# Expert routing with integer indices read in place, one mask table, two expert tables, and the negation and the gates on ScalarE

## The reference, cut to what matters

```
top_s, top_i = lax.top_k(scores, PEER_TOPK)
cand = (top_s[..., 0, :, None] + top_s[..., 1, None, :]).reshape(..., 256)
best_s, best_j = lax.top_k(cand, PEER_TOPK)
i1 = take_along_axis(top_i[..., 0, :], best_j // 16); i2 = take_along_axis(top_i[..., 1, :], best_j % 16)
experts = i1 * PEER_KEYS + i2
gates = jax.nn.softmax(best_s, axis=-1)
act = gelu(einsum('td,tkd->tk', h, u_tab[experts])); out = einsum('tk,tkd->td', gates * act, v_tab[experts])
```

## Time and profile before

| what | value |
|---|---|
| time, median of 3 runs | 1670.06 us (1668.13 to 1670.81) |
| the profiled execution's own time | 1670.59 us |
| its span, first to last instruction | 1668.8 us |
| busy: PE, DVE, ACT, POOL | 1308.3, 1209.0, 432.8, 677.2 us |
| moved by DMA | 623.21 MB, of which gathers 536.90 MB |

### The profile page before, as it was taken

How to read it: one execution, slowest core, us unless ns; L and a number is a source line. 1 busy time by engine, 2 the same in 40 slices (tenths; PEclk the granted TensorE clock), 3 DMA queues, 4 the chain that set the end, 5 groups by cost and what they waited for, 6 DMA issues and landing times. The chain is left out here.

```text
span 1668.8 us, 15094 instructions
## 1 busy us (share of the span) xinstructions
PE 1308.3 (78%) x4636; PEld 732.2 (44%) x4636; DVE 1209.0 (72%) x2831; ACT 432.8 (26%) x1021; POOL 677.2 (41%) x791
## 2 busy tenths in 40 slices
PE   7794776977696697878878777889878788776786
PEld 6664432433354344544355434545345433332332
DVE  3834999865599978767589987867679975555555
ACT  3211331341233321224133332135123321111111
POOL 6002223686175253344333243434432235444441
PEclk9898998988798898988989888989989979999999
DMA  9006998969998899999999999999999989999998
GB/s 387 18 29 265 418 374 334 392 258 367 421 407 351 328 420 419 420 421 419 420 398 420 411 345 420 420 419 420 420 401 420 402 319 422 420 419 420 420 420 334
DMA packets 86050, 623.21 MB, mean 373 GB/s; under 512 B 9808, under 2 KB 9808, under 8 KB 10960
## 3 DMA queue, kind: packets, MB, share of 16 engines
q0 software_dynamic: 73728, 536.90, 78.9%
q1 hardware_dynamic: 12240, 85.33, 12.5%
HBM read 621.15 MB, written 1.05 MB: 373 GB/s over the span
## 5 line engine op out<-in xcount | busy, mean ns | idle before, releaser
L1348 PE MATMUL acc<-slot,diag 128*128 128x512 f32 x1780 | 870.1, 644 | 226.9 <-ACT diag L734 226.9
L458 POOL DMA_INDIRECT slot<-experts,idx x512 | 577.9, 1129 | 950.3 <-PE acc L1348 785.4
L1041 DVE CUSTOM_DVE_ANT_0 slot<-slot,h 128x1024 f32<-128x1024 f32 x512 | 611.8, 1226 | 273.1 <-DMA slot<-experts,idx 271.5
L1348 PEld LDWEIGHTS acc<-slot,diag 128*128 128x128 f32 x1780 | 358.1, 207 | 689.4 <-issue 419.8
L734 ACT ACTIVATE diag<-cst,ge 128x128 f32<-128x128 f32 x445 | 144.2, 391 | 187.0 <-DVE ge L760 185.8
L725 ACT ACTIVATE ge<-ge 128x4 f32<-128x4 f32 x129 | 26.5, 205 | 466.0 <-DVE ge L1041 465.1
L1318 PE MATMUL PB<-hT,ring 128*128 128x128 f32 x1024 | 126.2, 284 | 4.6 <-ACT hT L698 4.1
L1318 PEld LDWEIGHTS PB<-hT,ring 128*128 128x128 f32 x1024 | 122.8, 200 | 6.5 <-ACT hT L698 5.5
L719 ACT ACT_TABLE_LOAD x31 | 39.8, 1283 | 203.1 <-DVE rs L1000 203.1
L1059 DVE SCALAR_TENSOR_TENSOR xs<-slot,ge,xs 128x1024 f32<-128x1024 f32 x67 | 86.1, 1285 | 2.4
L725 ACT ACT_TABLE_LOAD x56 | 71.8, 1283 | 29.3 <-DVE ge L1041 28.4
(11 more groups left out here) (229 smaller groups left out, 1148.4 us busy)
## 6 DMA issues: line engine op xcount, KB each, us to landing
ring<-weights SPq DMA_DIRECT2D x32, 1152.0 KB, 9.5
ring<-weights SPq DMA_DIRECT2D x28, 1024.0 KB, 9.2
slot<-weights SPq DMA_DIRECT2D x12, 1024.0 KB, 22.2
slot<-experts,idx POOLq DMA_INDIRECT x512, 16.1
sml<-small SPq DMA_DIRECT2D x2, 1160.0 KB, 10.0
xs<-x SPq DMA_DIRECT2D x2, 512.0 KB, 8.1
out<-xs SPq DMA_DIRECT2D x4, 256.0 KB, 5.1
tabp<-tabs SPq DMA_DIRECT2D x2, 268.0 KB, 9.2
```

What stands on the lines that cost most here:

```text
L458: pool.indirect_dma_start(out=slot[:, E % SLOTS, :], out_offset=None, in_=experts, in_offset=bass.IndirectOffsetOnAxis(ap=idx[:, n % 2, e: ...
L1041: ins = dve.tensor_tensor_reduce(u, u, h2[:, n % 2, :], 1.0, 0.0, ALU.mult, ALU.add, d[:, i:i + 1])
L1348: ins = pe.matmul(acc[:, half, :], diag[:, d % DIAGS, :], slot[:, E % SLOTS, D + half * 512:D + half * 512 + 512], start=(E % PICKS == 0), ...
```

## The change

Each part of it is in `route` or beside it:

- The reference to one expert table is replaced by two, `experts0` and `experts1`, one for each layer, and `gather` takes the one of its step. The offset (L1015) goes; the multiply-add (L1014) writes the indices itself.
- `bj` is split by one bitwise AND with a constant pair of rows (240 and 15) instead of a shift and an AND. The constants are written by two memsets on POOL at the start. The first half is then 16 times i1's place, and the table that it is compared with holds 0, 16, ..., 240 for the first half and 0 to 15 for the second.
- The conversions to float (L1003, L1006) go: comparison and product read the uint32 tiles as they are.
- The negation (L1000) is done by ACT, ahead of its exponential; the last MAX8 itself signals `top_ready`.
- The gates (L1019) are done by ACT: it waits behind the exponential for DVE's reciprocal (`ginv_ready`), multiplies, and signals `gated`. DVE waits for `gated` in the first quad of every head.

```diff
-def trunk(nc, x, consts, small, tabs, weights, experts, out):
+def trunk(nc, x, consts, small, tabs, weights, experts0, experts1, out):
@@ POOL
+            pool.memset(parts[:, 0, :], (TOPK - 1) * TOPK)
+            pool.memset(parts[:, 1, :], TOPK - 1).then_inc(S["parts_ready"], 1)
...
+                src = experts[n // TILES]
...
-                        out=slot[:, E % SLOTS, :], out_offset=None, in_=experts,
+                        out=slot[:, E % SLOTS, :], out_offset=None, in_=src,
@@ ACT, route
                 act.wait_ge(S["top_ready"], R + 1)
+                link(act.activation(rs[:, 0:1], bs[:, 0, 0:1], ACT.Copy, scale=-1.0))
                 told(act.activation(bs[:, 1, :], bs[:, 0, :], ACT.Exp, bias=rs[:, 0:1],
                                accum_out=rs[:, 1:2]), "gexp_ready")
+                act.wait_ge(S["ginv_ready"], R + 1)
+                told(act.activation(gate[:, n % 2, h * TOPK:(h + 1) * TOPK], bs[:, 1, :], ACT.Copy,
+                               scale=rs[:, 2:3]), "gated")
@@ DVE, route
-                def best():
-
-                    told(dve.tensor_scalar(rs[:, 0:1], bs[:, 0, 0:1], -1.0, None, ALU.mult), "top_ready")
-
-                top16([(bs[:, 0, :], bj[:, 0, :], cand[:, 0, :], cand[:, 1, :])], best)
-                lag(dve.tensor_copy(tif[:, :, :], ti[:, :, :]))
-                lag(dve.tensor_scalar(bj[:, 1, :], bj[:, 0, :], 4, None, ALU.logical_shift_right))
-                link(dve.tensor_scalar(bj[:, 2, :], bj[:, 0, :], 15, None, ALU.bitwise_and))
-                link(dve.tensor_copy(bjf[:, :, :], bj[:, 1:3, :]))
+                top16([(bs[:, 0, :], bj[:, 0, :], cand[:, 0, :], cand[:, 1, :])], "top_ready")
+                if R == 0:
+                    dve.wait_ge(S["parts_ready"], 1)
+                link(tt(bj[:, 1:3, :], bj[:, 0, :].unsqueeze(1).to_broadcast([P, 2, TOPK]), parts[:, :, :],
+                        ALU.bitwise_and))
...
-                link(tt(hot, bjf[:, :, :].unsqueeze(3).to_broadcast(both),
-                        c_("iota").unsqueeze(1).unsqueeze(1).to_broadcast(both), ALU.is_equal))
-                link(tt(hot, hot, tif[:, :, :].unsqueeze(2).to_broadcast(both), ALU.mult))
+                place = c_("iota").rearrange("p (i a) -> p i a", i=2).unsqueeze(2).to_broadcast(both)
+                link(tt(hot, bj[:, 1:3, :].unsqueeze(3).to_broadcast(both), place, ALU.is_equal))
+                link(tt(hot, hot, ti[:, :, :].unsqueeze(2).to_broadcast(both), ALU.mult))
                 link(dve.tensor_reduce(ex[:, 0:2, :], hot, AX.X, ALU.add))
-                link(dve.scalar_tensor_tensor(ex[:, 2, :], ex[:, 0, :], float(KEYS), ex[:, 1, :], ALU.mult, ALU.add))
-                told(dve.tensor_scalar(idx[:, n % 2, h * TOPK:(h + 1) * TOPK], ex[:, 2, :], float(l * EXPERTS), None,
-                                       ALU.add), "routed")
+                told(dve.scalar_tensor_tensor(idx[:, n % 2, h * TOPK:(h + 1) * TOPK], ex[:, 0, :], float(KEYS),
+                                              ex[:, 1, :], ALU.mult, ALU.add), "routed")
                 dve.wait_ge(S["gexp_ready"], R + 1)
-                link(dve.reciprocal(rs[:, 2:3], rs[:, 1:2]))
-                link(dve.tensor_scalar(gate[:, n % 2, h * TOPK:(h + 1) * TOPK], bs[:, 1, :], rs[:, 2:3], None,
-                                       ALU.mult))
+                told(dve.reciprocal(rs[:, 2:3], rs[:, 1:2]), "ginv_ready")
@@ DVE, weigh
                 dve.wait_ge(S["gelu_ready"], G + 1)
+                if quad % PER_HEAD == 0 and quad < QUADS:
+
+                    dve.wait_ge(S["gated"], PH * n + quad // PER_HEAD + 1)
```

More of the change, by code:

```diff
@@ L42 @@
 QUADS = PICKS // GRP
+PER_HEAD = TOPK // GRP
 DIAGS = 6
@@ L53 @@
 for _name, _w in (("ident", P), ("mask", P), ("ones", P), ("band", 4 * P), ("prev", 64), ("first", 64),
-                  ("iota", TOPK), ("minus", HEADS), ("eps", 1)):
+                  ("iota", 2 * TOPK), ("minus", HEADS), ("eps", 1)):
     CONST[_name] = (_at, _at + _w)
@@ L194, in by_vector @@
     return E - by_tensor(E)
-def trunk(nc, x, consts, small, tabs, weights, experts, out):
+def trunk(nc, x, consts, small, tabs, weights, experts0, experts1, out):
     ctx = ExitStack()
     with ctx:
+        experts = (experts0, experts1)
         def sb(name, shape, dt=F32):
@@ L291, in trunk @@
         ti = sb("ti", [P, 2, TOPK], U32)
-        tif = sb("tif", [P, 2, TOPK])
+        parts = sb("parts", [P, 2, TOPK], U32)
         bs = sb("bs", [P, 2, TOPK])
         bj = sb("bj", [P, 3, TOPK], U32)
-        bjf = sb("bjf", [P, 2, TOPK])
-        ex = sb("ex", [P, 3, TOPK])
+        ex = sb("ex", [P, 2, TOPK])
         rs = sb("rs", [P, 4])
@@ L316, in trunk @@
                  "merged_ready", "x1_ready", "sumsq_x1", "rms_x1", "h2_ready", "h2T_psum",
-                 "h2T_ready", "qT_psum", "qTs_ready", "sc_ready", "top_ready", "gexp_ready", "routed",
+                 "h2T_ready", "qT_psum", "qTs_ready", "sc_ready", "parts_ready", "top_ready", "gexp_ready", "ginv_ready", "gated", "routed",
                  "dots_ready", "gelu_ready", "w_ready", "diag_ready", "expert_done", "added", "drained",
@@ L604, in dt, with gate_ @@
                 told(act.activation(base[:, 0, :], t_("ldt"), ACT.Exp), "dt_ready")
-            def gate(n):
+            def gate_(n):
                 act.wait_ge(S["pf_psum"], n + 1)
@@ L735, in weigh @@
                                    scale=ge[:, 2, G % 2, i:i + 1]).then_inc(S["diag_ready"], 1)
-            run(dict(dt=dt, normA=normA, gate=gate, ln=ln, bT=turn_b, z=z, glu=glu, qkn=qkn, v=v, att=att, pool=pool_, sq=sq,
+            run(dict(dt=dt, normA=normA, gate=gate_, ln=ln, bT=turn_b, z=z, glu=glu, qkn=qkn, v=v, att=att, pool=pool_, sq=sq,
                      merge=merge, x1=x1_, h2T=h2T, rp=rp, route=route), lambda n, quad: None, weigh)
@@ L965, in x1_, with top16 @@
                                                   ALU.mult), "h2_ready")
-            def top16(pairs, after=None):
+            def top16(pairs, found=None):
                 step = lag if len(pairs) == 2 else link
@@ L974, in top16 @@
                 for vals, inds, src, scratch in pairs:
-                    step(dve.max(vals[:, 8:16], scratch))
-                if after:
-                    after()
+                    ins = dve.max(vals[:, 8:16], scratch)
+                    if found:
+                        told(ins, found)
+                    else:
+                        step(ins)
                 for vals, inds, src, scratch in pairs:
@@ L1382, in const_pack @@
     put("first", first.reshape(P, -1))
-    put("iota", np.arange(TOPK)[None, :])
+    put("iota", np.concatenate([np.arange(TOPK) * TOPK, np.arange(TOPK)])[None, :])
     put("minus", -np.eye(P, HEADS))
@@ L1465 @@
     i = {k: np.asarray(v) for k, v in inputs.items()}
+    rows = [np.concatenate([i["peer_u"][l], i["peer_v"][l]], 1) for l in range(DEPTH)]
     small, tabs = small_pack(i)
@@ L1472 @@
         "weights": weight_pack(i),
-        "experts": np.concatenate([i["peer_u"], i["peer_v"]], 2).reshape(DEPTH * EXPERTS, 2 * D),
+        "experts0": rows[0],
+        "experts1": rows[1],
     }
```

## The result

| kernel | median | runs | against the kernel before, 95% interval |
|---|---|---|---|
| before | 1669.1 us | 1665.75 to 1670.81 | |
| changed | 1696.55 us | 1694.68 to 1698.05 | 1.0169 [1.0156, 1.0182] |

The change makes the kernel slower by 27.5 us; forecast were 1695.1 us and slower with 0.84. The profiled execution took 1697.49 us; its span is 1695.6, 26.8 more than before.

A forecast was written before the change was run, and what follows sets the result against it. DMA bounds most of the run, DVE's chain the stretches around the routings. First gather -0.9, step 0 +5.6, step 1 +7.0, steps 2 and 3 +12.8: +24.5 on 1670.59 gives 1695.1 us, range 1680 to 1707.

The forecast's parts named there:

- the four stretches: Around the routings: DVE waits for no gather for some 150 to 170 us, so its chain sets the run time.
- w: DVE's gate product, which waits for ACT's Gelu in a routing quad: forecast at t0 + 5.67, before t0 + 4.87.
- a hiding DMA: Rival: gathers in flight cover DVE's lag, only the first routing step counts, 1669.7 us; chance 0.06.
- The quad: One routing quad: 0.80 us longer, Gelu and its table load standing behind the gates, despite 1.15 us less DVE work.
- The quad with "bT": Quad of "route6", where ACT's copy of 512 columns is no longer covered: 1.40 us longer instead of 0.80.
- the rival with another 1.38 us of emptying: Rival: an exposed table switch on ACT costs 1.38 us more, 31 times, 1738 us; chance 0.02.
- The index work: DVE's routing chain: conversions, shift and AND save 0.48 us, the offset 0.21 us.
- The uint32 rival: Rival: a uint32 operand halves the rate of DVE's comparison and product, 0.69 us longer each, 1739 us; chance 0.03.
- Step 1's routing: Routing quads of step 1: 7 x 0.80 + 1.40, together +7.0 us.
- The bound of 1.8 less for this place: Step 1's routing, where DVE meets POOL's rotation-table run: earlier delays absorbed, four quads costing 1.4 us, not 3.2.
- The first gather: First routing step: the gather waiting for the index write comes 0.19 + 0.48 + 0.21 = 0.88 us earlier.
- The rival in which the Gelu's load goes first: Rival: ACT loads the Gelu's table ahead of its wait for the reciprocal, 1654.5 us; chance 0.07.

The follow-up runs named there:

- the gates alone: Kernel before with only the gates moved to ACT behind DVE's reciprocal, nothing else of the change; 1719.95 us, ratio 1.0288.
- seven copies: Kernel before with seven dead copies of 16 columns on ACT between exponential and Gelu of every routing step; 1702.69 us, ratio 1.0197.

## Why the prediction was right

**The bound.** DVE's chain set the pace in the four stretches: DVE's delay is found again in the span, +25.7 at the last routing quad and +26.8 at the end. The windows with 315 and 285 GB/s, though, are not ones in which DVE is full (13.24 and 13.60 of 20). The routings' last products w start inside them, at 966.41 and 1349.32, and in the first DVE then waits 6.1 us for PE's sums. The full DVE is in the windows ahead of them (19.34 at 940 us). The reading was right, the rows for it were not the best. The chance of 0.06 for a hiding DMA was fair: between kernels that are faster than before DMA does hide part.

**The quad.** Forecast +0.80, measured +0.85 from the MAX8 to w in the quad shown, +0.88 a quad in step 0 and +0.85 in step 2 (14.01 to 14.85). The reciprocal was right to 0.01. Two hand-overs on the path came 0.02 longer each than in the rows they were priced from (the reciprocal's end to ACT 0.10 for 0.08, the Gelu's start to w 0.31 for 0.29). That is the 0.05, and times 31 it is some 1.6 us. The quad with "bT" behind its routing step was 1.50 longer, where 1.40 was forecast.

**The table load.** It was the largest piece of the Gelu's lateness: without it the quads of step 0 are 1.28 us shorter, and the run 39.1. Its price when exposed is the same 1.28 as when hidden, and the next instruction starts 0.01 behind it, so the rival with another 1.38 us of emptying falls. "ScalarE: Activation LUTs" of the Trainium skill puts a switch at about 2.66 us; nothing here shows its second half.

**The index work.** Forecast were -0.48 and -0.21, together -0.69 a quad, measured -0.64 in step 0. The uint32 rival falls.

**Step 1's routing** was mis-sized: +7.0 forecast, +9.3 measured, and the excess lies in one quad, 27 (w's delay goes from 6.95 to 10.09, where 0.8 was forecast). The last of POOL's runs, which the prediction looked at, cost about what it did before (the AND 6.0 us over its usual 0.19, the multiply-add 6.4 over 0.17). DVE met it at the AND and not, as put there, at the product, and nothing was absorbed: POOL's run did not keep its place in time but began 6.2 us later itself (524.64 for 518.42). What was left out is the run before it. In the old kernel it began at 509.29, as the dot products (1.22 each) ended, and stood beside DVE's searches. In the changed kernel it began at 512.00, just ahead of the dot products, which took 1.65, 1.63, 1.64 and 3.00 us: 3.0 us more. That the run is what stretched them is read from the timelines; no experiment took this one away. The bound of 1.8 less for this place had the wrong sign.

**The first gather** was issued 0.50 us earlier (143.41 for 143.91), not 0.88, since the last MAX8 itself was 0.31 later (139.16 for 138.85; in the kernels with the gates on DVE and with the Gelu first it was 1.2 and 1.0 earlier, so that looks like scatter of the start and not like the change). Not even the 0.50 arrived: the fourth expert's dot product could start at 160.74, before at 160.53. With the +0.85 of its quad that makes the +1.1 at quad 0, where -0.1 was forecast.

**The end** took 1.1 us that the forecast had at nothing. Twelve microseconds of it in the changed kernel, up to PE's last matmuls, by engine:

```profile
1680.00:1692.00 12.00, 11.59 (x24) 4.63 (x22) 7.76 (x13) 1.25 (x5) 0.00 (x0) 0.86 0.37 152
```

The granted clock was 0.86 of full speed in it: for most of the stretch from 1680 to 1684 it stood at the lower level, 1.2 GHz (0.55 and 0.60 in the two halves), with PE's weight loads 0.85 us apart instead of 0.43. PE had been busy for 7.16 of the 10 us ahead of it, at 1.00. The kernel before had 1.00 in the same place (1653 to 1665 us). DVE then waited 1.11 us for PE's last matmuls, for which it did not wait before. One execution of each shows it; it was not tested.

**The total** is closer than its parts. The sum starts from an execution 1.5 us above the median of the kernel before, so that 1695.1 lies 1.5 below the measured median, while the added time was +24.5 against 27.5. Up to quad 0 the forecast was 1.2 us short, in the rest of step 0 0.5, in step 1 2.3, in steps 2 and 3 together 0.3, at the end 1.1: 5.4 in all. The 3.1 us that the difference loses again between the routings were at nothing in the forecast and hide more than half of this. What they come from stays open, and that they came is luck.

The rival in which the Gelu's load goes first did not come of itself, but its place was the right one: with load and Gelu put there by hand the kernel takes 1648.56 us.

## What to carry to other kernels

Before moving a small operation to an idle engine, look at what is queued behind it there: an in-order queue makes everything behind the moved operation wait for its input too, a table load above all, and here 1.15 us less work on the busy engine became some 0.85 us more time in each of 31 quads. An operation that nobody needs soon (the gates) goes behind the one that somebody waits for (the Gelu). And when a cover is thought to be 1.4 us long, dead copies put into it, shorter than it in one run and longer in another, tell whether it is there.

The same change with the Gelu issued first, or with the gates left on DVE, beats both kernels: 1648.56 and 1649.52 us against 1669.1 and 1696.55. Below that a routing quad meets DMA: four experts and a chunk of weights are 5.37 MB, by estimate 12.8 us at the 420 GB/s of the windows.

## What was not expected of the hardware

In each of the eleven profiled kernels that compute the whole rotation table, one DVE instruction was held for 6.1 to 7.3 us until POOL's last run on the table was over: the multiply-add for 6.59 us before, for 6.61 with the gates on DVE and with the Gelu first, the AND for 6.21 in the changed kernel, a cast for 7.00 with the gates alone, the product for 7.25 with seven copies. The run is six POOL instructions, and DVE got in between none of them. "SBUF — State Buffer" of the Trainium skill (section "SBUF: two separate sides") gives the port pair that the two engines share to the one that starts first, for that whole instruction, and has the other block. The trace agrees that DVE blocks, but here the block lasts for a run of six.

The dot products beside the run before it met something milder: 1.63 to 1.65 us for three of them instead of 1.22, while POOL's pairs of instructions took 2.19 and 3.17 us instead of 1.38 and 1.20. No experiment separates the two forms, and none shows that the ports are the cause; the kernel without POOL's last run shows only that the long stall goes with it.
